# A scheduled PSUM copy of modulation rows on ScalarE is moved one unit earlier in an encoder step's first feed-forward block

## The reference

```
mod = silu(c) @ w_mod + b_mod                 # c: 1 prompt row and 8 sample rows; w_mod is 1024 x 9216
sh1, sc1, gt1, sh2, sc2, gt2, sh3, sc3, gt3 = split(mod, 9)
x = x + 0.5 * gt1 * swiglu(rms(x) * (1 + sc1) + sh1, w_gate, w_up, w_down)       # first feed-forward block
x = x + gt2 * mixer(rms(x) * (1 + sc2) + sh2)                                    # attention and delta net
x = x + 0.5 * gt3 * swiglu(rms(x) * (1 + sc3) + sh3, w_gate2, w_up2, w_down2)    # second feed-forward block
y = rms(x) * norm_final
```

## Time and profile before

| | us |
|---|---|
| median of 3 runs | 1543.74 |
| the three runs | 1541.65 to 1543.97 |
| the profiled execution's own time | 1539.34 |
| its span, first to last instruction | 1537.5 |
| PE busy in it | 1450.8 (94% of the span) |
| DVE busy | 885.4 (58%) |
| ACT busy | 573.9 (37%) |
| POOL busy | 394.7 (26%) |
| mean granted TensorE clock | 0.977 of full |

### The profile page before, as it was taken

How to read it: one execution, slowest core, us unless ns; L and a number is a source line. 1 busy time by engine, 2 the same in 40 slices (tenths; PEclk the granted TensorE clock), 3 DMA queues, 4 the chain that set the end, 5 groups by cost and what they waited for, 6 DMA issues and landing times. The chain is left out here.

```text
span 1537.5 us, 28532 instructions
## 1 busy us (share of the span) xinstructions
PE 1450.8 (94%) x11426; PEld 1350.9 (88%) x11430; DVE 885.4 (58%) x1637; ACT 573.9 (37%) x1130; POOL 394.7 (26%) x360
## 2 busy tenths in 40 slices
PE   5899999999999989998997889999899999999996
PEld 3789999999999989987895668689899999999995
DVE  2636665575467451666576556573557548754863
ACT  3532332333243342653324424542544224422443
POOL 1702421331232240531002030112713024302400
PEclk9999999999999989999999989999899999999998
DMA  9424445445343323322106020233113312331221
GB/s 343 129 82 138 151 139 163 137 154 162 124 152 100 82 56 78 91 69 56 42 1 150 11 76 27 70 90 96 55 42 96 97 52 85 92 103 44 86 78 69
DMA packets 211736, 148.76 MB, mean 97 GB/s; under 512 B 18075, under 2 KB 190396, under 8 KB 211608
## 3 DMA queue, kind: packets, MB, share of 16 engines
q1 hardware_dynamic: 206264, 129.15, 28.7%
q0 software_dynamic: 5344, 17.81, 3.7%
HBM read 139.99 MB, written 6.95 MB: 96 GB/s over the span
## 5 line engine op out<-in xcount | busy, mean ns | idle before, releaser
L1005 PE MATMUL pair<-b_hi,w_hi 128*128 128x320 f32 x720 | 224.6, 312 | 0.0
L1005 PE MATMUL pair<-b_hi,w_lo 128*128 128x320 f32 x720 | 222.7, 309 | 0.0
L1005 PE MATMUL pair<-b_lo,w_hi 128*128 128x320 f32 x720 | 222.6, 309 | 0.0
L1075 PE MATMUL pair<-act_hi,w_hi 128*128 128x320 f32 x704 | 162.0, 311 | 0.0
L1075 PE MATMUL pair<-act_lo,w_hi 128*128 128x320 f32 x704 | 160.6, 309 | 0.0
L1075 PE MATMUL pair<-act_hi,w_lo 128*128 128x320 f32 x704 | 160.5, 309 | 0.0
L471 DVE SCALAR_TENSOR_TENSOR x_t<-pair,gate,x_t 128x320 f32<-128x320 f32 (+1 forms) x128 | 56.0, 479 | 167.1 <-PE pair L1075 141.6
L1005 PEld LDWEIGHTS pair<-b_hi,w_hi 128*128 128x128 f32 x720 | 135.2, 188 | 14.2 <-DVE w_lo L594 8.4
L588 ACT ACTIVATE w_hi<-sums_a 128x512 fp32r<-128x512 f32 x72 | 45.1, 627 | 251.9 <-POOL sums_a L622 132.0
L890 DVE TENSOR_TENSOR uvw<-pair,uvw 128x320 f32<-128x320 f32 (+1 forms) x126 | 67.7, 537 | 123.0 <-PE pair L1005 122.6
L1005 PEld LDWEIGHTS pair<-b_lo,w_hi 128*128 128x128 f32 x720 | 135.2, 188 | 0.0
(11 more groups left out here) (424 smaller groups left out, 3162.3 us busy)
## 6 DMA issues: line engine op xcount, KB each, us to landing
w_mod_raw<-w_mod SPq DMA_DIRECT2D x28, 1024.0 KB, 5.8
w_raw<-ffn_w_gate SPq DMA_DIRECT2D x40, 512.0 KB, 4.0
raw_more<-ffn_w_up SPq DMA_DIRECT2D x40, 512.0 KB, 3.8
w_raw<-w_in SPq DMA_DIRECT2D x24, 512.0 KB, 3.7
w_raw<-ffn_w_down SPq DMA_DIRECT2D x16, 384.0 KB, 3.3
raw_more<-ffn_w_down SPq DMA_DIRECT2D x16, 384.0 KB, 3.2
w_mod_a<-w_mod POOLq DMA_DIRECT2D x4, 1024.0 KB, 10.9
w_mod_b<-w_mod POOLq DMA_DIRECT2D x4, 1024.0 KB, 24.2
```

Source lines behind the costliest of these rows:

```text
L1005: mm = pe.matmul(job_bank(j, BANK_OF[part]), w[:, at, kk], mv[:, kk, s], start=(kk == 0 and v == 0 and part in FIRST_OF_BANK), stop=(kk == ...
L1075: mm = pe.matmul(pair[part % 2][:, b, 0:HALF], w[:, slot, k], mv[:, k, b * HALF:(b + 1) * HALF], start=(k == 0 and v == 0), stop=(k == n - ...
```

## The change

The table entry that places ScalarE's copy of step 0 is now item 4 and no longer item 5. No other entry of the four tables changes, since `at < 4` holds for one entry alone (at = 3).

```diff
@@ mod_steps()
     for n, at in enumerate(spots[:2 * LATER_STEPS]):
         rows[at] = divmod(n, 2)
         if n % 2:
-            late = at + (2 if ITEMS[0][at][4] == 2 and ITEMS[0][at + 2][4] == 2 else 3)
+            late = at + 1 if at < 4 else at + (2 if ITEMS[0][at][4] == 2 and ITEMS[0][at + 2][4] == 2 else 3)
             out[late] = n // 2
             turn[spots[n + 1]] = n // 2
             place[spots[n + 1] + 1] = n // 2
```

## The result

The changed kernel takes 1533.64 us (median of 7 runs, 1530.79 to 1538.22) against 1543.66 us (7 runs, 1541.00 to 1546.80) of the kernel before: a ratio of 0.9940 with a 95% interval of 0.9921 to 0.9958, or some 9 us of gain, give or take 3. The profiled execution took 1530.79 us and was the fastest of the seven; its span was 1529.0 instead of 1537.5.

The account below looks back on a forecast made before the run. PE was taken to bound the kernel, standing still for ScalarE's late copy. Standstill 3.82, turn and half step 0.98 and unit 6 0.68 sum to 5.48 us: 1543.74 - 5.5 = 1538.2 us, range 1535.0 to 1541.0.

Parts of the forecast that it names:

- The standstill: PE idle ahead of modulation step 0's turn, waiting for ScalarE's copy of `mod_row`; removing it was to save 3.82 us.
- The half step and unit 6 at full clock: PE work behind step 0's turn, slow after the idle; turn and half step to give 0.98 us, unit 6 0.68.
- The move past the weight split: ScalarE's copy goes ahead of a weight split, which starts some 0.5 us later, covered by 5.01 us of idle; cost 0.
- Nothing was late next: Loads of `w_mod` and inputs of units 6 and 7 arrive in time; the next load keeps 8.9 us of slack.
- the place: PE from the end of unit 5 through step 0's turn, half step and unit 6; the whole 5.48 us was summed there.
- Rival 1: Light work of turn and half step lowers the clock even without a standstill; only 3.8 us gained, 1539.9 us; chance 0.08.
- rival 2: Gain absorbed later by a transfer or VectorE holding PE; with half stuck 2.7 us left, 1541.0 us; chance 0.10.
- rival 4: The copy isn't what holds PE, another wait ends at the same moment; no change, 1543.7 us; chance 0.02.
- the clock term: Faster matmuls in turn, half step and unit 6 once TensorE stays at its upper level; 1.66 us, called least certain.
- its two bounds: Gain between 3.82 us, the standstill alone, and 7.6 us, with the lower level lasting twice the idle time.
- I take nothing off for it: All stages behind the change slide forward with the same waits, so the whole 5.48 us lasts to the end.
- Rival 3: Later stages, beginning 5.5 us earlier, are granted less clock; with 17 us more at the lower level 1546.7 us; chance 0.03.

Follow-up runs that it names:

- hold8: Kernel before with 8 unread matmuls on PE ahead of its wait for the copy, filling the standstill; pooled 4.4 +- 1.2 us below the kernel before.
- hold: Kernel before with 16 unread matmuls on PE ahead of its wait for the copy, turn 2.96 us later; 1.8 +- 1.9 us below the kernel before.
- refill: Changed kernel with 25 unread matmuls on PE right ahead of the turn of step 0, which starts 10.9 us later; 1545.9 +- 2.2 us.
- refill13: Changed kernel with 13 unread matmuls on PE right ahead of the turn of step 0, which starts 5.7 us later; 1540.83 +- 1.76 us.
- half_way: Kernel before with the copy moved only ahead of item 5's four copies, 2.23 us of idle left; 2.5 +- 1.9 us below the kernel before.
- norm_fill: Changed kernel with unread matmuls in three PE waits of each of the two norm stages; 1533.96 +- 1.48 us against 1534.06 +- 1.01.

## Why the prediction was right and wrong

**Right, step by step.** The standstill was ScalarE's copy alone: turn start 93.14 (forecast 93.18). The half step and unit 6 at full clock: unit 7 starts at 102.16 (102.2). The move past the weight split cost nothing: 0.48 us out of an idle of 5.01. Nothing was late next: the load behind is issued at 95.16 (95.2). In the pair of executions on which the sum was made, the place is worth 5.5 us, as summed. (The unit of 7.14 us in that sum is unit 4, from 79.01 to 86.15; the forecast calls it unit 3, and the number is right.) Rival 1 (the clock falls anyway) is excluded by hold8 and by the changed kernel's own traces, rival 2 (absorbed later) by a gain in the mean that is larger than the place's, and rival 4 by the result.

**Wrong: the clock term, first at the place.** What failed is one term of the sum, the clock. It was put at 1.66 us at the place and at nothing later; measured, it is 2.3 us at the place and 2.2 +- 1.3 later, and the standstill of 3.8 us was right. "What the clock gives back (0.98 + 0.68 = 1.66 us)" was read from one execution and carried over to the median: "For the median I take the same difference." That execution was 4.4 us below the median, which was named and not used. Five traces give 2.3 us on average; the profiled one has the smallest loss of the five, together with the fifth (21.92 and 21.94 us). The rule of the Trainium skill that I quoted (TensorE: Matmul & The Clock Gate, Part 1: The HAM clock gate), that such a loss differs from run to run, is said there of the start of a kernel; the traces agree with it for a fall in the middle of one: 1.65 to 2.9 us. The forecast said that by this rule the sum was anything between its two bounds, and yet took the one row as the value.

**Wrong: "I take nothing off for it", and nothing added.** The forecast held the later stages to slide rigidly. They did in their instructions and waits, but not in their clock. Of the 8.3 us, 6.1 arise at the place and 2.2 +- 1.3 later, where the kernel before has falls at 855 to 865 us in five of five traces and the longer ones at 890 to 930. Rival 3 named this mechanism, but as a loss only, with a chance of 0.03. A change of the later stages' clock should have stood on both sides of the forecast. The range ended at 1535.0, which is the bound of 7.6 us of gain and 1.1 us for the spread of the runs, and so left no room for it. In means the miss adds up: 1538.2 was forecast and 1534.1 measured, of which 1.4 us is that the three runs' median of 1543.74 stood above the mean of the kernel before (1542.35), 0.6 the place and 2.2 the later stages.

**What stays open.** The kernels without the fall at 97 us spend less time at the lower level (hold, hold8, refill and the changed kernel 73 to 74 us, refill13 77.6) than the kernel before (84.5) and half_way, which keeps the fall (80.3). Of the 10.8 us between the two kernels, 5.5 lie at the place. When these 5.5 are taken off the kernel before, 79.0 are left, and only the changed kernel and hold8 lie below that by more than their interval. Why the later falls are rarer isn't settled. The earlier position of the later stages (P) isn't excluded: in hold8 they begin only 2.2 us earlier on average and yet another 2.2 +- 1.4 us are gained later, which speaks against it, but a small shift may be enough; and hold, whose stages begin no earlier, gains 2.5 +- 1.9 us beyond the place's 2.3 of clock by the pooled figures and 1.9 +- 2.1 within its set. That the missing fall makes the later ones rarer (F) isn't shown either: the means of hold8 and of hold speak for it, and most single traces speak against it, as the table of the stretch from 845 to 960 us shows. refill13, meant to decide between the two, lies between both forecasts.

## What to carry to other kernels

A standstill of the matrix engine cost its own length and then the slow clock behind it, here 3.8 and 2.3 us at the place; the whole change gave 8.3 us, and why it gave 2.2 more than the place isn't known. With 1.4 us of the standstill taken away the clock still fell, and 2.5 +- 1.9 us were gained. Look for a small instruction on another engine that the matrix engine waits for and whose own input was ready long ago: here it had been for 17 us, and one table entry was enough. And price clock terms from several executions: the clock losses of one trace are not those of the median, and a gain of a few microseconds needs dozens of executions where the same program differs by 5. Where executions fall in two groups, give the mean beside the median.

## What the runs showed of the hardware

An fp32 matmul of 128x256 results takes 0.44 us at the upper clock level (16 records in 3.6 us are 8 of them); I had expected half. Matmuls that nobody reads kept the clock up through a wait of 3.8 us (hold8, granted clock 1.00 from 98 to 107 us), and through norm stages that have 5.7 and 6.9 us of idle without them (1.00 instead of 0.74 in two of three traces of norm_fill, 0.91 in one stage of the third). Less time at the lower level is not less time in total: 17.6 +- 6.1 us less of it, in norm_fill, moved the mean by 0.1 +- 1.8 us. And the same work of one program, from 845 to 960 us in the kernel before, took from 111.3 to 118.7 us in five traces of the changed kernel, with nothing in the program different.
